# Modulation chunks summed four at a time in a PSUM bank of their own, beside a ring of seven banks

## The reference

```
mod   = jax.nn.silu(c) @ w_mod[layer] + b_mod[layer]            # 1024 -> 6 * 1024
sh1, sc1, g1, sh2, sc2, g2 = jnp.split(mod[:, None, :], 6, axis=-1)
mod_c = jax.nn.silu(c_ctx) @ w_mod[layer] + b_mod[layer]
h = rmsnorm(x, gain) * (1 + sc1) + sh1
x = x + g1 * mix(h);  x = x + g2 * swiglu(modulate(x, gain2, sh2, sc2), w_ffn_in, w_ffn_out)
```

## Time and profile before

| | |
|---|---|
| three runs | 2066.52, 2066.03, 2059.63 us; median 2066.03 |
| the profiled execution | 2062.51 us, its span 2060.4 us |
| granted TensorE clock, mean | 0.964 of full speed |
| busy: TensorE, VectorE, ScalarE, GpSimd | 92%, 48%, 38%, 24% of the span |
| HBM traffic | 259.00 MB read, 126 GB/s over the span |

### The profile page before, as it was taken

One profiled execution on the slowest core, in us unless ns is written; L12 is line 12 of the kernel. 1 busy time (PEld: TensorE's weight loads), 2 busy tenths in 40 slices (PEclk: granted clock), 3 DMA queues, 4 the chain that ended last, 5 costly groups with the idle time before them and its releaser, 6 DMA issues.

```text
span 2060.4 us, 31602 instructions
## 1 busy us (share of the span) xinstructions
PE 1894.3 (92%) x13332; PEld 1617.1 (78%) x13332; DVE 998.4 (48%) x1628; ACT 785.6 (38%) x1330; POOL 495.2 (24%) x234
## 2 busy tenths in 40 slices
PE   5998999989989999998899869999999989689999
PEld 2777898878979999786686646888888767468999
DVE  1648535555354333545776774222222246964343
ACT  2453522333325555431532233322222234655443
POOL 0135213321213434111230001212121212013443
PEclk7998999999999999999999979999999999999999
DMA  7443343222065554422120023232333236115553
GB/s 299 173 154 129 117 150 117 83 103 83 27 248 195 190 188 163 144 82 86 69 83 21 1 103 123 102 123 104 122 110 115 102 133 231 56 49 200 188 193 128
DMA packets 36571, 262.08 MB, mean 127 GB/s; under 512 B 4048, under 2 KB 4176, under 8 KB 6224
## 3 DMA queue, kind: packets, MB, share of 16 engines
q1 hardware_dynamic: 36432, 260.07, 34.7%
HBM read 259.00 MB, written 1.05 MB: 126 GB/s over the span
## 4 chain that ended last, share of the span: by engine, by line
PE 74%; DVE 14%; ACT 4%; issue 3%; DMA 2%; POOL 2%; SPq 0%; DVEq 0%; ACTq 0%
PE ps L766 17%; PE ps L768 17%; PE ps L767 17%; PE ps L1010 2%; PE ps L793 2%; PE ps L1021 2%; PE ps L839 2%; PE ps L1027 2%; POOL wl L686 1%; PE ps L817 1%; PE ps L1220 1%; PE ps L1223 1%; ACT wh L1327 1%; PE ps L783 1%; DVE msq L2237 1%
## 5 line engine op out<-in xcount | busy, mean ns | idle before, releaser
L686 POOL TENSOR_TENSOR wl<-raw,wh 128x1024 fp32r<-128x1024 f32 (+1 forms) x179 | 428.1, 2394 | 1346.7 <-ACT wh L1327 1346.7
L766 PE MATMUL ps<-h_hi,wh 128*128 128x256 f32 (+1 forms) x1696 | 551.4, 325 | 7.3 <-POOL wl L686 5.1
L768 PE MATMUL ps<-h_hi,wl 128*128 128x256 f32 (+1 forms) x1696 | 543.7, 321 | 0.0
L767 PE MATMUL ps<-h_lo,wh 128*128 128x256 f32 (+1 forms) x1696 | 542.2, 320 | 0.0
L1327 ACT ACTIVATE wh<-raw 128x1024 fp32r<-128x1024 f32 (+1 forms) x330 | 342.4, 1040 | 400.2 <-PE ps L768 292.3
L766 PEld LDWEIGHTS ps<-h_hi,wh 128*128 128x128 f32 x1696 | 320.5, 189 | 36.4 <-POOL wl L686 9.7
L767 PEld LDWEIGHTS ps<-h_lo,wh 128*128 128x128 f32 x1696 | 320.4, 189 | 27.5 <-issue 2.4
L768 PEld LDWEIGHTS ps<-h_hi,wl 128*128 128x128 f32 x1696 | 319.8, 189 | 25.6
L1811 DVE TENSOR_TENSOR wl<-raw,wh 128x1024 fp32r<-128x1024 f32 (+1 forms) x151 | 187.9, 1244 | 236.0 <-ACT wh L1327 235.8
L766 PE MATMUL ps<-gh,wh 128*128 128x256 f32 (+1 forms) x528 | 171.5, 325 | 0.0
L768 PE MATMUL ps<-gh,wl 128*128 128x256 f32 (+1 forms) x528 | 167.4, 317 | 0.0
(11 more groups left out here) (392 smaller groups left out, 3007.6 us busy)
## 6 DMA issues: line engine op xcount, KB each, us to landing
raw<-in_mod SPq DMA_DIRECT2D x72, 1024.0 KB, 4.8
raw<-in_ffn_in SPq DMA_DIRECT2D x66, 1024.0 KB, 4.8
raw<-in_ffn_out SPq DMA_DIRECT2D x24, 1024.0 KB, 4.8
raw<-in_w_in SPq DMA_DIRECT2D x16, 1024.0 KB, 4.8
raw<-in_w_gate SPq DMA_DIRECT2D x12, 1024.0 KB, 4.8
raw<-in_w_ab SPq DMA_DIRECT2D x12, 1024.0 KB, 4.8
raw<-in_ffn_out SPq DMA_DIRECT2D x12, 768.0 KB, 4.3
raw<-in_w_at SPq DMA_DIRECT2D x5, 1024.0 KB, 5.1
```

Of the source, the lines that this page charges most:

```text
L686: nc.gpsimd.tensor_tensor(wl[e % SPLIT][:, 0:entries[e]["words"]], part(e), wh[e % SPLIT][:, 0:entries[e]["words"]].bitcast(F32), ALU.subt ...
L766: nc.tensor.matmul(b[:, cols], wh[e % SPLIT][:, w], xh(k), start=(k == 0), stop=False)
L767: nc.tensor.matmul(b[:, cols], wh[e % SPLIT][:, w], xl(k), start=False, stop=False)
L768: ins = nc.tensor.matmul(b[:, cols], wl[e % SPLIT][:, w], xh(k), start=False, stop=(k == nk - 1))
```

## The change

The ring has 7 banks. The eighth is `modsum`: four chunks (`SET`) are summed in it one behind the other. They don't mix since each chunk's two columns land on rows of their own: the two columns of `cvec` stand in a strip of 14 columns that are zero otherwise, and chunk j of the set takes a window of 32 columns that starts 2 * (3 - j) into it. TensorE counts finished chunks in `mod_read`; SP waits for it before it loads a raw buffer again, and ScalarE waits for it behind the fourth chunk, when it copies all four at once (`mod_rows`). The first chunk of a set waits on TensorE for that copy of the set before. The pick is made once per set, at the calls with n = 4, 8, ..., 72, with 8 columns for 2, and VectorE adds the biases in two instructions for a set.

```diff
-BANKS = 8
+BANKS = 7
+SET = 4
+STRIP = 4 * SET - 2
-for _name, _w in (("cvec", 32), ("bmod", 144), ("gain", 48), ("fing", 8), ("bgate", 24), ("dconv", 36),
+for _name, _w in (("cvec", 16 * STRIP + 32), ("bmod", 144), ("gain", 48), ("fing", 8), ("bgate", 24), ("dconv", 36),
...
             if n < MODS:
                 chunk("mod", n)
-                direct([("modrow", n)])
-            if 0 < n <= MODS:
-                add("modcol", n - 1)
+                chunks[-1]["last"] = -1
+            if n > 0 and n % SET == 0:
+                add("modcol", n // SET - 1)
...
-    ps = nc.alloc_psum_tensor("ps", [P, BANKS, 512], F32)
+    ps = nc.alloc_psum_tensor("ps", [P, BANKS + 1, 512], F32)
...
                 w = slot("mod", n)
-                b = begin("modrow", n)
-
+                g, j = n // SET, n % SET
+                if j == 0 and g > 0:
+                    pe.wait_ge(sem("mod_rows"), g)
+                b = modsum()
                 for k in range(KD):
-                    j = k % 4
-                    o = SMALL["cvec"][0] + 16 * min(n // 24, 1) + 2 * k
-                    ins = nc.tensor.matmul(b[32 * j:32 * j + 32, 0:256], small[:, o:o + 32],
-                                           w[:, 256 * k:256 * k + 256], start=(k < 4), stop=(k >= 4),
-                                           skip_group_check=True)
-                close(ins)
-            if 0 < n <= MODS:
-                evacuated(pe, "modrow", n - 1)
-                b = begin("modcol", n - 1)
+                    i = k % 4
+                    o = SMALL["cvec"][0] + STRIP * (8 * min(n // 24, 1) + k) + 2 * (SET - 1 - j)
+                    ins = nc.tensor.matmul(b[32 * i:32 * i + 32, :], small[:, o:o + 32],
+                                           w[:, 256 * k:256 * k + 256], start=(j == 0 and k < 4),
+                                           stop=(j == SET - 1 and k >= 4), skip_group_check=True)
+                ins.then_inc(sem("mod_read"), 1)
+            if n > 0 and n % SET == 0:
+                g = n // SET - 1
+                pe.wait_ge(sem("mod_rows"), g + 1)
+                b = begin("modcol", g)
...
-                if n < MODS:
-                    full(act, "modrow", n)
-                    free(A(modrow[:, n % 2, :], bank("modrow", n)[:, 0:256], ACT.Copy), "modrow", n)
+                if n < MODS and n % SET == SET - 1:
+                    g = n // SET
+                    act.wait_ge(sem("mod_read"), n + 1)
+                    if g > 0:
+                        full(act, "modcol", g - 1)
+                    A(modrow[:], modsum(), ACT.Copy).then_inc(sem("mod_rows"), 1)
```

More of the change, by code:

```diff
@@ L658, in _ @@
                 old = chunks[n - RAW]
-                if old["last"] is not None:
+                if old["name"] == "mod":
+                    sp.wait_ge(sem("mod_read"), old["i"] + 1)
+                elif old["last"] is not None:
                     sp.wait_ge(psum_full, old["last"] + 1)
@@ L811, in mod_one @@
                 w = slot("mod", n)
[L812 removed]
+                g, j = n // SET, n % SET
+                if j == 0 and g > 0:
+                    pe.wait_ge(sem("mod_rows"), g)
+                b = modsum()
                 for k in range(KD):
[L815 to L823 removed]
+                    i = k % 4
[8 more added lines that the diff above has]
+                b = begin("modcol", g)
                 for i in range(2):
[L825 to L826 removed]
+                    ins = nc.tensor.matmul(b[:, 2 * SET * i:2 * SET * i + 2 * SET], modrow[:, P * i:P * i + P],
+                                           S("pick"), start=True, stop=True)
                 close(ins)
@@ L1821, in mod @@
                 modn[0] += 1
-                if 0 < n <= MODS:
-                    n -= 1
+                if n > 0 and n % SET == 0:
+                    n = n // SET - 1
                     full(dve, "modcol", n)
-                    lay, c = n // 24, n % 24
+                    lay, c = SET * n // 24, SET * n % 24
                     o = 48 * lay + 2 * c
-                    bias = S("bmod")[:, o:o + 2].unsqueeze(2).to_broadcast([P, 2, 2])
-                    free(V.tensor_tensor(mods[:, lay, 2 * c:2 * c + 2, :],
-                                         bank("modcol", n)[:, 0:4].rearrange("p (m v) -> p m v", m=2), bias,
-                                         ALU.add), "modcol", n)
-                    if c in (7, 19):
+                    for m in range(2):
+                        bias = S("bmod")[:, o + m:o + m + 2 * SET - 1:2].unsqueeze(2).to_broadcast([P, SET, 2])
+                        ins = V.tensor_tensor(mods[:, lay, 2 * c + m:2 * c + m + 2 * SET - 1:2, :],
+                                              bank("modcol", n)[:, 2 * SET * m:2 * SET * m + 2 * SET].rearrange(
+                                                  "p (j v) -> p j v", v=2), bias, ALU.add)
+                    free(ins, "modcol", n)
+                    if c + SET - 1 in (7, 19):
                         evacuated(dve, "modcol", n)
+                        c += SET - 1
                         i = 2 * lay + (c == 19)
@@ L2546, in layout @@
     cv[:, 1, :, 1] = _feat(a["c_ctx_2"])
-    put("cvec", cv.reshape(P, 32))
+    strips = np.zeros((P, 16, STRIP), f)
+    strips[:, :, 2 * (SET - 1):2 * SET] = cv.reshape(P, 16, 2)
+    put("cvec", np.concatenate([strips.reshape(P, 16 * STRIP), np.zeros((P, 32), f)], 1))
     put("bmod", np.concatenate([_feat(a["b_mod"][0]), _feat(a["ada_b_2"][0]), _feat(a["ada_b_2"][1])], 1))
@@ L2575, in layout @@
     put("sink", np.broadcast_to(a["attn_sink_2"][0][heads], (P, 16)))
-    pick = np.zeros((P, 2), f)
+    pick = np.zeros((P, 2 * SET), f)
     for j in range(4):
-        for v in range(2):
+        for v in range(2 * SET):
             pick[32 * j + v, v] = 1.0
```

9 lines of the change are left out of this document (6 added, 3 removed).

## The result

The changed kernel took 2079.51 us in the median of five runs (2077.06 to 2088.08), the kernel before, run beside it, 2066.52 (2059.63 to 2068.17). The ratio is 1.0078 with a 95% interval of 1.005 to 1.0105: slower by 0.8%, where 0.7% faster was forecast. The five runs lie in two groups, 2077.1 to 2079.5 and 2086.2 to 2088.1. The profiled execution is of the upper one (2086.16 us, span 2084.4, clock 0.961), so that its trace shows some 7 us more than the median does. Of all executions in this document one, of the kernel before with seven banks and MA first, took 3711 us; it is in no ratio.

What follows compares the result with a forecast made beforehand. TensorE, busy 1894.3 of 2060.4 us, was taken as the bound. Terms 2.35 + 2.35 + 1.0 + 0.5 + 9.4 + 1.9 - 4.9 - 1.5 = +11.1 took 2062.5 to 2051.4, forecast as 2052; range 2044 to 2068.

Steps and rivals of the forecast that it cites:

- The small operand is 230 columns wider: Opening, 22 to 46: 118 KB more to load, 0.3 us if on the path; the opening counted 0.
- What seven banks cost: mLSTM: MS waits for mout and L2311, making MN later, -4.9 us; more low clock there and at the norms, -1.5.
- The delta stage: Four steps: dropped picks and bank waits, earlier Y in steps 2 and 3, +9.4 us in all, bounds +3 and +13.
- so I count 0 for that while the clock stays up: Delta stage, set's end: X0T behind the chunk that waits for ScalarE's copy costs 0, since X0T waits for X anyway.
- The third rival: Slower, by the clock at the set's end: gaps of 2.3 us drop the clock, time 2072 us; chance 0.11.
- The rule against this change: Every new wait ahead of TensorE's bursts would lose the clock, giving the third rival's sum; forecast kept only -1.5 us.
- the conv stretch: 66 to 130 us: five pick pairs leave a gapless TensorE, 0.47 us each, +2.35.
- the feed-forward: First feed-forward term: five of seven sprinkled pick pairs go, +2.35 us.
- no gain at the norms: Norms of a2, b1, b2, c1, c2: pick pairs lie under VectorE's chain, so dropping them gives 0.
- Ahead of w_o: Near 597 us: two pick pairs go and no new one comes, +1.0.
- the attention: Fewer ScalarE copies between conversions, a late pick gone, fewer adds: +1.9 us, bounds 0 and 4.
- it cancels: Rival: half the delta gain stays, 4.7 us, and seven banks cost 12.8; sum 0, time 2062.5; chance 0.23.

Runs made afterwards that it cites:

- seven banks and MA first: Kernel before with BANKS = 7 and the mLSTM tiles MA and ME made ahead of the pair MS: 2076.9 us, ratio 1.0049.
- 24 words: Changed kernel with 24 unused words (96 bytes) a partition behind the small operand, activations starting at 64 modulo 128 as before: 2070.4 us, ratio 1.0016.
- 16 and 24 words: The one with 16: changed kernel with 16 unused words (64 bytes) behind the small operand: 2086.2 us, ratio 1.0098; 24 words has its own line.
- the set's end moved out of the step: Changed kernel with 24 words, plus one modulation chunk moved from ahead of w_dn_out to the conv stretch: 2068.5 us, ratio 1.0002.
- 8 words: Changed kernel with 8 unused words (32 bytes) a partition behind the small operand: 2074.3 us, ratio 1.0038.
- the order that shortened the waits with eight banks: Kernel before, eight banks, with mLSTM tiles MA and ME made ahead of the pair MS: 2074.3 us, ratio 1.005.
- the kernel with seven banks: Kernel before with BANKS = 7, one PSUM bank unused, nothing else: 2087.3 us, ratio 1.0093.

## Why the prediction was wrong

- **The place in SBUF** was in no term. "The small operand is 230 columns wider" was costed as a transfer, and not as what moves all tensors behind it. It is 13 us of the result (give or take 7): 1.0078 against 1.0016 with nothing but the place put back. Without it the change is even with before (2070.4 beside 2068.0, 1.0016), not faster, and 18 above the forecast.
- **What seven banks cost** was forecast as -4.9 and -1.5 for the clock; it measured 19 by itself. The place and the mechanism were right for the mLSTM (MS behind mout and L2311, one tile ahead of where MA stood), its size was short: 6.7 in the trace of the changed kernel, in which the clock mostly stayed up, and 12.4 in the trace with 24 words, in which MS and MA ran low. The sentence that failed is "Of its 819 tiles most don't notice": with the list of before, the delta stage lost 9.0 too. There the waits were for the modulation's own adds, and the changed kernel has none of these; how much of the rest it still pays no run tells apart.
- **The delta stage**, +9.4, gave 1.2 in this trace and 0.3 with 24 words: -0.5, -0.8, +2.6 and 0 by steps, for +0.9, +0.9, +4.6 and +3.0 (the first two are small for one trace, but those with 16 and 24 words have nearly the same). The wait of KQ for mods went as forecast. Two steps of the reasoning failed. The first is "so I count 0 for that while the clock stays up": X0T stands behind the chunk's wait of 2.2 to 2.5 us and comes 0.8 late even at the high level, 2.0 in step 0 at the low one. The third rival had this wait (2.3) and mechanism; it put X0T 2.5 late. With the set's end moved out of the step the stage is 5.1 shorter, so the two terms were real and nearly cancelled. The second is that Y's earlier start was taken to carry to the end of the step: in step 3 Y came 4.1 earlier (3.0 forecast) and 2.3 of that went to waits behind it, where VectorE now sets the pace.
- **The rule against this change**, the Trainium skill's page "TensorE: Matmul & The Clock Gate", section "A second HAM failure mode: psum-queue depth-cycling" (a clock that swings with the small idle gaps of a kernel that cycles through PSUM banks), covers a part of this and not its main part. The rows agree with it at three of the four set ends in this trace and at none with 8 words, where the waits are the same and the stage still gains only 2.1. It does not tell where the clock falls: step 3 has the longest wait and stayed up here but not with 24 words, and the order that shortened the waits with eight banks had the lowest clock.
- **Right**: the conv stretch (2.35 forecast, 2.3 measured), the feed-forward (2.35 and 2.2), no gain at the norms. Ahead of w_o 0.3 was measured for 1.0 (1.1 were won at the two pairs, and a new wait of 0.65 us stands 6 us behind them), in the attention a loss of 0.5 for +1.9, and with 24 words a gain of 2.9; two traces of one kernel differ by up to 1.8. In the retention the loss of 2.7 is one stretch of low clock (951.5 to 958), where the order waits no longer than before. The sum of the gains, 17.5 before the ring's cost, is close to the 16.9 that the runs give for the modulation by itself, and that is luck in part: against the kernel with seven banks the delta stage is 7.6 shorter in the trace, but in steps 1 and 3 (3.4 and 2.8), where seven banks had made the waits for the modulation's adds longer, and by 0.9 in step 2, for which 4.6 had been forecast.
- **The rivals**: "it cancels" gave the time of the kernel with its place put back (1.0016), in part by luck: the delta stage gave 0.3 for its 4.7, the attention 2.9 for 1.9 in that trace. Its 12.8 for seven banks, put on the mLSTM, was near that stretch's 12.4. None of the rivals had the place.

## What to carry to other kernels

When a change makes a tensor longer or shorter, write down where each tensor behind it starts, before and after, and keep the start of what TensorE streams where it was: here 32 or 96 bytes cost 0.6 to 0.9% and showed in no busy time, wait or clock, only in the distance from one dense matmul to the next. Taking a bank from a ring can cost in stages that nobody had listed (here 9.0 us in the delta stage): list for each tile what it waited for and waits for now, in the stages that have gaps already, and then look whether another order of tiles makes the wait harmless (here -0.5% with seven banks, but +0.5% with eight). A wait that is added in front of work of one engine is free only if nothing behind it feeds the chain that sets the stage.

## What the runs showed of the hardware that was not expected

- The interval of float32 matmuls of 512 columns (three products of split operands) was 226.9, 228.9 and 233.3 ns for activations that start at 0, 64 and 32 or 96 bytes modulo 128; with 256 columns 120.0, 117.8, 116.7 (at 32) and 118.3 or 120.0 (at 96). Only these places were tried, with the weights at a multiple of 128; which memory or port is behind it was not tried.
- With 256 columns, 113.3 and 117.8 ns came at the same place in two traces of the same program (240 to 540 us).
- The same gaps of 2.2 to 2.5 us in the delta stage were followed by the low clock in steps 0, 1 and 2 of the changed kernel's trace, in steps 0, 2 and 3 with 24 words and in none with 8 words. The five runs of the changed kernel fall into two groups some 9 us apart.
